# Stage ends and stage starts worked token tile by token tile, with six split and four raw weight slots, in a three-layer fp32 transformer kernel

## Time and profile before

| | |
|---|---|
| median of 3 runs | 1188.71 us (1186.17 to 1189.02) |
| span of the profiled execution | 1185.7 us, first to last instruction |
| that execution's own time | not listed apart; its span lies 3.0 us under the median |
| PE busy | 1039.1 us, 88% |
| DVE busy | 797.3 us, 67% |
| ACT busy | 519.8 us, 44% |
| DMA | 219.63 MB, mean 185 GB/s |
| mean granted PE clock | 0.942 |

### The profile page before, as it was taken

How to read it: one execution, slowest core, us unless ns; L and a number is a source line. 1 busy time by engine, 2 the same in 40 slices (tenths; PEclk the granted TensorE clock), 3 DMA queues, 4 the chain that set the end, 5 groups by cost and what they waited for, 6 DMA issues and landing times.

```text
span 1185.7 us, 14582 instructions
## 1 busy us (share of the span) xinstructions
PE 1039.1 (88%) x4856; PEld 857.0 (72%) x4856; DVE 797.3 (67%) x1118; ACT 519.8 (44%) x762; POOL 123.5 (10%) x114
## 2 busy tenths in 40 slices
PE   2599667999999887796999999599999879999996
PEld 2488456788878665675888787488877667888785
DVE  6768977677777789767555584745654655777653
ACT  1344453444443333434444433347454534555441
POOL 1100931000000066201000000200000010000001
PEclk9799779999999978897999999799999999999998
DMA  8987613688878834233666776366533344565540
GB/s 299 326 298 252 191 36 124 201 260 269 275 275 320 291 128 157 89 100 92 199 183 188 248 248 173 109 195 194 159 109 125 124 142 144 176 180 174 177 142 36
DMA packets 136775, 219.63 MB, mean 185 GB/s; under 512 B 9075, under 2 KB 77928, under 8 KB 136728
## 3 DMA queue, kind: packets, MB, share of 16 engines
q1 hardware_dynamic: 135440, 216.05, 56.2%
q0 software_dynamic: 960, 2.86, 0.8%
q10 hardware_dynamic: 328, 0.12, 0.0%
HBM read 217.94 MB, written 1.05 MB: 185 GB/s over the span
## 4 chain that ended last, share of the span: by engine, by line
PE 79%; DVE 12%; ACT 3%; DMA 2%; POOL 2%; issue 1%; SPq 0%; POOLq 0%; DVEq 0%; ACTq 0%
PE bank L1499 16%; PE bank L1501 16%; PE bank L1500 16%; PE bank L1514 8%; PE bank L1516 7%; PE bank L1515 7%; DVE w_lo L859 2%; PE bank L1528 1%; DVE wgt L1109 1%; PE bank L1539 1%; DMA ada<-in_ada_w 1%; DMA raw<-in_a_w_qkv 1%; POOL stat L415 1%; DVE ada_acc L880 1%; ACT w_hi L518 1%
## 5 line engine op out<-in xcount | busy, mean ns | idle before, releaser
L859 DVE TENSOR_TENSOR w_lo<-raw,w_hi 128x1024 fp32r<-128x1024 f32 x312 | 385.3, 1241 | 302.8 <-ACT w_hi L518 300.0
L518 ACT ACTIVATE w_hi<-raw 128x1024 fp32r<-128x1024 f32 x312 | 328.7, 1059 | 485.9 <-PE bank L1501 306.0
L1499 PE MATMUL bank<-w_hi,h_hi 128*128 128x512 f32 x848 | 340.7, 402 | 13.2 <-DVE h_lo L930 13.0
L1501 PE MATMUL bank<-w_hi,h_lo 128*128 128x512 f32 x848 | 334.0, 394 | 0.0
L1500 PE MATMUL bank<-w_lo,h_hi 128*128 128x512 f32 x848 | 333.4, 393 | 0.0
L1499 PEld LDWEIGHTS bank<-w_hi,h_hi 128*128 128x128 f32 x848 | 161.6, 191 | 48.7 <-issue 8.9
L1501 PEld LDWEIGHTS bank<-w_hi,h_lo 128*128 128x128 f32 x848 | 161.1, 190 | 34.8
L1500 PEld LDWEIGHTS bank<-w_lo,h_hi 128*128 128x128 f32 x848 | 161.6, 191 | 32.6 <-issue 0.5
L880 DVE SCALAR_TENSOR_TENSOR ada_acc<-ada,cond,ada_acc 128x512 f32<-128x512 f32 x140 | 104.9, 749 | 7.1 <-DMA ada<-in_ada_w 3.6
L1514 PE MATMUL bank<-w_hi,u_hi 128*128 128x512 f32 x264 | 106.4, 403 | 3.3 <-DVE act_u L1140 2.6
L1516 PE MATMUL bank<-w_hi,u_lo 128*128 128x512 f32 x264 | 103.5, 392 | 0.0
(11 more groups left out here) (220 smaller groups left out, 1036.3 us busy)
## 6 DMA issues: line engine op xcount, KB each, us to landing
ada<-in_ada_w SPq DMA_DIRECT2D x96, 512.0 KB, 5.2
raw<-in_f_w_in SPq DMA_DIRECT2D x176, 256.0 KB
raw<-in_w_in SPq DMA_DIRECT2D x46, 512.0 KB
raw<-in_f_w_out SPq DMA_DIRECT2D x44, 512.0 KB
raw<-in_w_up SPq DMA_DIRECT2D x88, 256.0 KB
raw<-in_a_w_qkv SPq DMA_DIRECT2D x24, 512.0 KB
raw<-in_w_down SPq DMA_DIRECT2D x22, 512.0 KB
raw<-in_b_w_qkv SPq DMA_DIRECT2D x12, 512.0 KB
```

The source lines that it names most:

```text
L518: nc.scalar.activation(w_hi[:, m % SPL], raw[:, m % RAW], ACT.Copy).then_inc(hi_done, 1)
L859: ve.tensor_tensor(w_lo[:, m % SPL], raw[:, m % RAW], w_hi[:, m % SPL].bitcast(F32), ALU.subtract).then_inc(lo_done, 1)
L1499: mm(o, hi, w_hi[:, s, k], start=(u == 0 and k == 0), stop=False)
L1501: last = mm(o, lo, w_hi[:, s, k], start=False, stop=(u == 3 and k == 1))
```

## The change

RAW falls from 8 to 4 and SPL rises from 4 to 6, in the same memory. Each stage's last four tall tiles (SKEW = 4; two in BR_B) are no longer run tile by tile but part by part: for each token tile t and output half n, all four tiles' matmuls into that bank, then a semaphore. DVE adds each 128x512 part as it is ready (`part_residual`), ACT squares each part (`part_square`, all squares are now ACT's), POOL's `root` works per token tile. ACT scales the first 512 columns and DVE the others (`part_scale`). PE turns the eight blocks of one token tile (`half_transposes`). The operand is made per token tile in four pieces of two 128-column blocks (`part_operand`): ACT writes `hf` (or `h_hi` directly where there is no shift), DVE the rest. `first_wide` runs the first four wide tiles of the next stage for token tile 0 and then for token tile 1. ACT and DVE split tiles nxt+2 to nxt+5 inside the boundary (nxt is the next stage's first tile). Between OUT_1 and IN_C the two norms are done from sums of squares of x and of x times `final_g`, and x itself is rescaled afterwards. OUT_C's eight tiles are two sets of four. The output is stored in four halves. All `Fori` loops are written out.

```diff
-RAW = 8
-SPL = 4
+RAW = 4
+SPL = 6
...
+            def last_tall(m0, a_hi, a_lo, k0, count=SKEW, base=0, only=False, between=None):
+                for t in range(T):
+                    for n in range(2):
+                        last = part_tall(m0, a_hi, a_lo, k0, count, t, n, base, only)
+                        if (t, n) != (T - 1, 1):
+                            last.then_inc(part_mm, 1)
+                        if (t, n) == (0, 1) and between is not None:
+                            between()
...
+            def first_wide(m0, o, src):
+                for t in range(T):
+                    for u in range(4):
+                        if t == 0 and u == 3:
+                            pe.wait_ge(half_lo, pieces_done(o, 0, 3))
+                            half_transposes(o, 1, src)
+                        pe.wait_ge(half_lo, pieces_done(o, t, u))
+                        pe.wait_ge(lo_done, m0 + u + 1)
...
+                        if t == T - 1:
+                            last.then_inc(mm_done, 1)
```

ACT's order at a stage end:

```diff
+            def boundary(r, o, nxt, gain, shift=None):
+                first = nxt - SKEW + SPL
+                for n in range(2):
+                    part_square(r, 0, n)
+                split(first)
+                part_scale(r, 0)
...
+                part_operand(o, 0, 0, gain, shift)
+                part_operand(o, 0, 1, gain, shift)
+                part_square(r, 1, 0)
+                part_square(r, 1, 1)
+                part_operand(o, 0, 2, gain, shift)
+                part_operand(o, 0, 3, gain, shift)
+                split(first + 1)
+                part_scale(r, 1)
```

DVE's order there, and one of the loops:

```diff
+            def boundary(r, s, o, nxt, gain, shift=None, gated=None, before=None):
+                part_residual(r, s, nxt, 0, 0, gated)
+                part_residual(r, s, nxt, 0, 1, gated)
+                if before is not None:
+                    before()
+                part_residual(r, s, nxt, 1, 0, gated)
+                part_scale(r, 0)
+                part_residual(r, s, nxt, 1, 1, gated)
+                part_operand(o, 0, 0, gain, shift)
+                part_operand(o, 0, 1, gain, shift)
+                low(first)
...
-            with v_.Fori(0, 5) as turn:
+            for turn in range(5):
```

More of the change, by code:

```diff
@@ L62, with pieces, pieces_done @@
 B_REDUCE, B_TAKE = {9: 0}, {10: 0}
+SKEW = 4
+def pieces(o):
+    return ((0, 4), (4, 8)) if o == 4 else ((0, 2), (2, 4), (4, 6), (6, 8))
+def pieces_done(o, t, p):
+    return sum(2 * len(pieces(n)) for n in range(o)) + t * len(pieces(o)) + p + 1
+OLD = {0: 0, 1: 1, 4: 2, 7: 3}
+HALF = D // 2
 SPATIAL_STEP, QK_STEPS = 26, (28, 29, 30)
@@ L84, in cols @@
 def cols(start, turn, per, size):
-    return slice(start, start + size) if turn is None else bass.ds(turn * per + start, size)
+    first = start if turn is None else start + turn * per
+    return slice(first, first + size)
 def program(nc, x_in, c_in, ada_w, ada_b, norm1_g, norm2_g, a_w_qkv, a_w_o, lq1, lk1, lq2, lk2,
@@ L296, in _ @@
                 load_wide(m, a_w_qkv[0], m % 4, m // 4 * CH)
-            with sp.Fori(0, 2) as turn:
+            for turn in range(2):
                 for j in range(LOOP):
@@ L310, in _ @@
                 load_ada(a)
+            for m in range(2, 4):
+                load_pair(IN_0 + m, f_w_in[0], m, 0)
             for m in range(8):
@@ L348, in _ @@
                 load_tall(OUT_1 + k, f_w_out[1], k)
-            with sp.Fori(0, 5) as turn:
+            for turn in range(5):
                 for j in range(LOOP):
@@ L648, in feed_forward @@
                 silu(base, f, 0, 0)
-                with act.Fori(0, 5) as turn:
+                for turn in range(5):
                     for j in range(LOOP):
@@ L712, in _ @@
             operand(4)
-            for m in range(WO_B, IN_1):
+            for m in range(WO_B, IN_1 - SKEW):
                 split(m + SPL)
-            square_0(3)
-            scale_0(3)
-            operand(5)
+            boundary(2, 2, IN_1, gains, mod[:, 72:80])
             act.wait_ge(setup_v, 2)
@@ L721, in _ @@
             feed_forward(IN_1, 1, 3)
-            square_0(4)
-            square_0(5)
-            scale_0(5)
-            operand(6)
-            with act.Fori(0, 2) as turn:
+            boundary(3, 3, IN_C, vecs[:, MIX_V:MIX_V + KD])
+            act.wait_ge(x_ok, 1)
+            for turn in range(2):
                 for j in range(LOOP):
@@ L789, in _ @@
             operand(7)
-            for m in range(BR_A, OUT_C):
+            for m in range(BR_A, BR_B):
                 split(m + SPL)
@@ L797, in _ @@
                     last.then_inc(sig_g, 1)
-            operand(8)
-            for m in range(OUT_C, UP_C):
+            for t in range(T):
+                for p in range(2):
+                    part_operand(4, t, p)
+                split(BR_B + t + SPL)
+            for m in range(OUT_C, UP_C - SKEW):
                 split(m + SPL)
-            square_0(6)
-            scale_0(6)
-            operand(9)
+            boundary(4, 5, UP_C, vecs[:, FFN_V:FFN_V + KD])
             def take_pair(c, b, turn=None):
@@ L981, in _ @@
+            affined = [0]
             v_.wait_ge(setup, 1)
@@ L1037, in _ @@
             PI_IN = float(np.nextafter(np.float32(math.pi), np.float32(0)))
-            operand(0, gains[:], mod[:, 0:8], then=lambda kk: kk < 3 and low(kk + 1))
+            operand(0, gains[:], mod[:, 0:8], then=lambda kk: low(kk + 1))
+            low(SPL - 1)
             minus_lambda()
-            with v_.Fori(0, 2) as turn:
+            for turn in range(2):
                 for j in range(LOOP):
@@ L1892, in av_transpose @@
                 last.then_inc(av_t, 1)
-            for u in range(4):
-                wide(UP_C + u, u, 0, 9, wait_operand=True)
-            with pe.Fori(0, 5) as turn:
+            first_wide(UP_C, 5, xn)
+            for turn in range(5):
                 for j in range(LOOP):
```

516 lines of the change are left out of this document (328 added, 188 removed).

## The result

| | before | after |
|---|---|---|
| median of the runs | 1187.78 us (4 runs) | 1157.91 us (1153.06 to 1160.67, 4 runs) |
| profiled execution: own time / span | not listed apart / 1185.7 us | 1156.39 / 1154.6 us |
| granted clock, mean | 0.942 | 0.967 |
| PE busy | 88% of the span | 90% |

The ratio is 0.9742, 95% interval 0.9724 to 0.976: 30 us faster, where 40 were forecast. The time lies inside the forecast range (1138 to 1170), above its likeliest value.

The account below looks back on a forecast made before the run. PE's own matmuls bound the kernel, so only stage ends could gain: 9.9 + 5.5 + 10.1 + 6.9 + 1.9 + 3.0 + 4.0 = 41.3 us, less 1.3 for loads, net 40; median 1148.7 us, range 1138 to 1170.

Parts of the forecast that it names:

- The loops at zero: Writing out all loops: a turn's jump back costs PE nothing visible in UP_C, so counted as 0.
- the rule that the prediction sets beside them: Skill's instruction-fetch rule for loops: a taken branch outside the two pages held stalls; would add one stall a turn.
- OUT_0 ... About 4 us come from waits that close. Bounds: 0 and the 6.8 us wait: OUT_0's end to QKV_B's attention: DVE keeps its work, closing waits gain 4 us.
- I charge 1.3 us: Cost of tighter weight and ada loading with four raw and six split slots: 1.3 us off the gain.
- the first eight QKV_A loads ... I charge nothing: Start of QKV_A: loads once issued together now wait for low parts; PE starts on tiles 0 to 3, so no cost.
- My slot turn of 9.4 us against 10.9: Raw slots: landing 5.2, split, fold and issue take 9.4 us, within four tile times of 10.9, 1.5 to spare.
- the sign I had named: Prediction counted as wrong if ACT waits for raw DMAs in IN_0 or OUT_0.
- raw slots starve: Rival, 4%: landing near 10.9 us makes QKV_A, IN_0 and OUT_0 lose 95 us, less 40: 1244.
- the clock falls anyway: Rival, 8%: granted clock 0.50 through token tiles 0 and 1 of four ends costs 19 us: 1168.
- a gain of 1.9: BR_B's end: 20.1 us before, 18.2 after, as DVE must first do four `merged` products.
- The other four rows of the table: Forecast gains at the ends of WO_A 5.5, WO_B 9.9, OUT_C 6.9 and DOWN_C 3.0 us.
- Two of the three signs by which I would have called the prediction wrong: ACT raw-DMA waits in IN_0 or OUT_0; PE waits over 3 us inside an end; QKV_B attention over 10 us nearer.

Follow-up runs that it names:

- two kernels with the same slots: The kernel before with loops written out, four raw and six split slots and old ends, 1194.37 us; against it the changed kernel, 1157.91 us.
- the two runs with folds of one column: POOL's folds of ada tiles 76 to 83 cut from 512 columns to one, sums left out: changed kernel 1133.02 us, kernel before 1170.36 us.
- the table run: Changed kernel with attention B's rope table loaded after OUT_0's tile 9 and made by DVE at OUT_0's step 14, not in QKV_B: 1152.07 us.

## Why the prediction was right or wrong

**Right: the kind of gain.** PE's own work bounds the kernel, and the gain came from the ends: 36 us between two kernels with the same slots. WO_A, WO_B and OUT_C took 14.4, 14.4 and 13.6 us to four tiles done, against forecasts of 18.3, 15.8 and 15.4; first matmuls came at T + 2.2, 2.2 and 1.6 (forecast "of 2 to 4 us"; OUT_1's came at T + 6.3, outside it), at clock 1.00. Two allowances were not needed there: POOL's root took 0.95 us from its start, not 2.4, and PE found token tile 1 scaled, so the gap of 1 to 2 us ahead of the second transposes is missing. At WO_A the reduction and the fold that I had set at 1.5 us before T cost 0.2 us of waiting and 0.9 of PE. ACT's affine pair took 0.75 us (four instructions in 1.50), above the 0.65 that I took and the 0.50 of the estimate beside it. The loops at zero were right. (Whether the condition of the rule that the prediction sets beside them was met, no trace shows, so the run does not test it.)

**Wrong by 9.2 us: the step "OUT_0 ... About 4 us come from waits that close. Bounds: 0 and the 6.8 us wait".** It measured -5.2. I took DVE's 61.97 busy us as work that stays, and asked only which waits would close. But 12.2 us of the 65.9 were POOL's folds, and it depends on the order of events which DVE instruction meets a fold. The folds came later in the changed kernel: POOL waits 9.6 us for ada tiles in this stretch, and 0 before. Then they met the table. The load of ada tile 76 stands in SP's queue behind that of QKV_B's tile 7, which with four raw slots waits for the low part of tile 3. The new end makes that low part inside the boundary, behind T (405.51):

```profile
414.53 1.23 DVE L977 TENSOR_TENSOR w_lo<-raw,w_hi 128x1024 fp32r<-128x1024 f32 x1 [0.19 <-ACT w_hi L575]
...
416.21 0.45 SPq L312 DMA_DIRECT2D ada<-in_ada_w  x1
```

With the old ends and the same slots it is made before T (413.31), and the load goes out 3.5 us before T:

```profile
409.79 0.45 SPq L284 DMA_DIRECT2D ada<-in_ada_w  x1
```

So the slots alone did not make the folds late, and with the new ends six raw slots do not cure it (POOL waits 10.5 us there): it is the low parts that the new end puts behind T, with loads queued behind them. I had counted these low parts as DVE's work (3.7 us) and not as what SP waits for. That the lower bound was nothing was wrong too: no reason excluded a loss. Seven of the 9.2 are measured by the two runs with folds of one column; the other 2.2 are the difference between 1.8 and 4.0, and their cause stays open. The three DMA issues ahead of POOL's root stood there before the change as well; the table run shows that moving them takes the first matmul from T + 5.6 to T + 2.2.

**Wrong by 2.8 us and more: "I charge 1.3 us" for the loads, "the first eight QKV_A loads ... I charge nothing".** QKV_A and attention A lost 4.1 us in the trace. The 2.2 of them before the first scores vary: the scores start at 119.7 before and at 121.9 here, but in five other traces of the same code up to there at 120.1, 120.1, 120.35, 120.4 and 123.9. Attention A's part is steady: 51.5 us before, 51.1 with six raw slots, and with four 53.3 to 53.5 in seven traces, that with the old ends among them, and 54.2 in an eighth. There POOL's first fold starts 3.0 us before the first scores in the kernel before (116.64) and 0.6 us after them in the changed one (122.49), so this too may be a matter of what DVE meets; no run separates it. With the old ends the slots cost 7 us in all. My slot turn of 9.4 us against 10.9 rested on the median landing; ACT now waits 6.9 us for raw tiles in QKV_A and 10.0 in IN_0, the sign I had named. The rival "raw slots starve" had the right place and too high a price: its 95 us needed every tile to be late, and seven in each stage were.

**Wrong by 4.3 us: BR_B** (forecast a gain of 1.9, measured -2.4), and by 2.0 at OUT_1, of which 1.2 are its end (19.6 against 18.4 us to four tiles done); where the other 0.8 are I did not find. The timeline at BR_B's end:

```profile
922.70 0.66 PE L1735 MATMUL bank<-ident,merged 128*128 128x128 f32 x4 [0.67 <-DVE merged L1560]
...
923.89 0.68 DVE L1107 TENSOR_TENSOR h_lo<-bank,h_hi 128x512 fp32r<-128x512 f32 x1
...
925.82 0.68 DVE L1107 TENSOR_TENSOR h_lo<-bank,h_hi 128x512 fp32r<-128x512 f32 x1
...
926.56 0.80 PE L1704 MATMUL bank<-w_hi,h_hi 128*128 128x512 f32 x1 [3.20 <-DVE h_lo L1107]
927.15 0.63 PE L1705 MATMUL bank<-w_lo,h_hi 128*128 128x512 f32 x1
```

PE starts on OUT_C's first four tiles only when the second piece's low part is done (926.50), though by the code these tiles read the chunks of the first piece alone, ready at 924.57. Behind that wait 14 matmuls run 0.43 us apart. The forecast had only the first two parts ready at T and missed this wait. The rival "the clock falls anyway" happened at OUT_1 (0.83), BR_B (0.85) and, for less, OUT_0 (0.92), where PE waited 4.0, 3.2 and 3.4 us, and at none of the ends where its wait was 1.3 us or less. (Its price of 19 us took 24 matmuls an end; four tiles have 48, which makes it 38.) At OUT_1, POOL's queue has two DMA issues that wait for T, ahead of the roots:

```profile
729.30 0.54 POOL L548 DMA_DIRECT2D mask_sb<-in_masks  x1 [180.39 <-PE bank L1706]
729.84 0.54 POOL L549 DMA_DIRECT2D gmlp_row<-in_gmlp_norm_g  x1
730.46 0.30 POOL L466 TENSOR_SCALAR stat<-stat 128x1 f32<-128x1 f32 x1
...
732.98 1.97 PE L1735 MATMUL bank<-ident,xs 128*128 128x128 f32 x8 [3.98 <-ACT xs L618]
```

ACT's last square for that root had been read out at 726.50, so the root starts 4.0 us later than it could. These two readings are argued from the trace; waiting for the first piece alone, and issuing the loads behind the roots, were not tried.

**Not forecast: attention B, 2.5 us.** Its eight transposes of `proj` take 1.97 us before and 1.10 after, so PE had the higher clock there (0.91 granted before and 0.97 after over the stretch); in the traces of all runs the stretch takes 54.2 to 63.0 us. I draw nothing from it.

The other four rows of the table, 2.9, 0.7, 2.3 and 0.9 us above forecast, are ends that took less than I had, with an earlier root and without the allowances named above. Together the misses are -9.2 - 2.8 - 4.3 - 2.0 + 2.9 + 2.5 + 0.7 + 2.3 + 0.9 = -9.0 us, the difference between the forecast's 40 and the 31 of the two spans. That the time fell into the range owes something to this: misses of 18.3 us one way and 9.3 the other. Two of the three signs by which I would have called the prediction wrong did show, ACT's waits for raw tiles in IN_0 and PE's waits over 3 us inside an end. And the forecast's own bounds, 1141 to 1157, do not come out of its terms: hand-overs of 0 to 1 us and 0 to 8 us in OUT_0 give about 1139 to 1153, with the measured 1157.9 above them.

## What to carry to other kernels

- A busy engine's time is not its own work until one has looked at its mean durations: the same form at 0.29 and 1.99 us in one trace is a wait that no wait list shows. Compare such a group's minimum with its mean before counting it as fixed.
- Work on POOL beside a bound DVE is not free help. The seven folds that fall between OUT_0 and attention B would take DVE 1.5 us each, 10.5 in all; made by POOL, they cost that stretch 19 us.
- When a stage's end is opened to the next stage, the slots that the last tiles hold until T decide the gain: count how many of the next tiles are ready at T. And look at what now waits behind T: a DMA issue in a queue ahead of the norm's root, or a load that stands behind a low part which the new order makes later.

## What the runs showed of the hardware

I had not expected how much DVE loses beside POOL. With POOL folding, DVE's product of 128x512 takes 2.08 us on the mean, and 0.68 where the folds have one column; a TENSOR_SCALAR on 4 columns 0.53 us and 0.17; one of attention A's `wgt` instructions 1.08 and 0.48. The reduction that reads PSUM keeps its time (0.677 and 0.682). A DVE instruction that meets a fold ends just behind it (421.34 + 1.99 against 421.00 + 2.17, and 427.06 + 1.98 against 426.85 + 2.04), so it looks blocked and not slowed (spans on POOL are rough in the profile, and this reading is no finer than they are). The Trainium skill, SBUF — State Buffer, Who interferes with whom, states this as a rule: VectorE and GpSimd share one pair of SBUF ports, taken as an exclusive lock for a whole instruction, by a VectorE instruction with two SBUF inputs against a GpSimd instruction that reads SBUF, or by a VectorE instruction in a two-port mode. The traces agree, with the numbers above.
